# Last two weight units of each stage taken row by row, small extractions moved behind the last product

## What is computed

```
def first_block(...):
    h = modulate(rmsnorm(x, g_norm1), sh1, sc1)
    ...
    o = concatenate([o_mla, o_ret], axis=-1) @ w_out
    x_new = x + gt1 * o
    x_new = x_new + gt2 * conv_ffn(modulate(rmsnorm(x_new, g_norm2), sh2, sc2), ...)
    return rmsnorm(x_new, g_final)
```

## Time and profile before

| | |
|---|---|
| median of 3 runs | 1185.05 us |
| lowest and highest run | 1183.73 and 1187.86 us |
| the profiled execution, its own time | 1186.22 us |
| its span, first to last instruction | 1184.4 us |
| mean granted TensorE clock | 0.990 of full speed |
| VectorE, ScalarE busy | 831.3 and 600.2 us |
| TensorE instructions | 7032 |

### The profile page before, as it was taken

One profiled execution on the slowest core, in us unless ns is written; L12 is line 12 of the kernel. 1 busy time (PEld: TensorE's weight loads), 2 busy tenths in 40 slices (PEclk: granted clock), 3 DMA queues, 4 the chain that ended last, 5 costly groups with the idle time before them and its releaser, 6 DMA issues.

```text
span 1184.4 us, 18112 instructions
## 1 busy us (share of the span) xinstructions
PE 1130.3 (95%) x7032; PEld 979.7 (83%) x7032; DVE 831.3 (70%) x899; ACT 600.2 (51%) x872; POOL 210.5 (18%) x164
## 2 busy tenths in 40 slices
PE   5899989999999998999989999998999998999997
PEld 1587758879999886899879999886878987999986
DVE  3796465778887968898666765966888778454533
ACT  4864354456655436444454444336556767444432
POOL 1037300005566302010001212200000000122200
PEclk9999999999999999999989999998999999999999
DMA  8685550148786886976547887874877334555551
GB/s 327 258 318 206 212 213 1 37 151 299 260 281 213 327 316 210 363 236 233 179 148 240 298 278 248 333 296 154 322 283 285 134 100 133 186 177 183 197 189 72
DMA packets 124303, 263.36 MB, mean 222 GB/s; under 512 B 8329, under 2 KB 76497, under 8 KB 114001
## 3 DMA queue, kind: packets, MB, share of 16 engines
q1 hardware_dynamic: 121553, 254.56, 60.8%
q0 software_dynamic: 2688, 7.95, 2.2%
HBM read 261.43 MB, written 1.05 MB: 222 GB/s over the span
## 4 chain that ended last, share of the span: by engine, by line
PE 78%; DVE 11%; ACT 4%; issue 3%; DMA 2%; SPq 1%; POOL 0%; DVEq 0%; ACTq 0%
PE ps L1843 23%; PE ps L1844 23%; PE ps L1845 23%; DVE wl L580 2%; DMA mod_w<-in_w_ada_dram 2%; PE ps L2136 1%; PE ps L2152 1%; ACT wh L1313 1%; PE ps L1878 1%; DVE vg L1108 1%; DVE acc L592 1%; DVE x L761 1%; DVE xn L757 1%; PE ps L2187 1%; PE ps L2195 1%
## 5 line engine op out<-in xcount | busy, mean ns | idle before, releaser
L580 DVE TENSOR_TENSOR wl<-raw,wh 128x2048 fp32r<-128x2048 f32 (+2 forms) x149 | 343.0, 2304 | 111.7 <-ACT wh L1313 111.0
L1843 PE MATMUL ps<-hh,wh 128*128 128x256 f32 (+1 forms) x1192 | 339.2, 285 | 7.2 <-DVE hl L738 3.4
L1313 ACT ACTIVATE wh<-raw 128x2048 fp32r<-128x2048 f32 (+2 forms) x148 | 279.0, 1890 | 130.9 <-DMA raw<-in_ffn_w_down_dram 53.1
L1844 PE MATMUL ps<-hl,wh 128*128 128x256 f32 (+1 forms) x1192 | 335.9, 282 | 0.0
L1845 PE MATMUL ps<-hh,wl 128*128 128x256 f32 (+1 forms) x1192 | 335.9, 282 | 0.0
L1843 PEld LDWEIGHTS ps<-hh,wh 128*128 128x128 f32 (+1 forms) x1192 | 225.0, 189 | 9.6 <-issue 5.7
L1844 PEld LDWEIGHTS ps<-hl,wh 128*128 128x128 f32 (+1 forms) x1192 | 225.0, 189 | 0.3
L1845 PEld LDWEIGHTS ps<-hh,wl 128*128 128x128 f32 (+1 forms) x1192 | 224.9, 189 | 0.2
L1843 PE MATMUL ps<-wh,hh 128*128 128x512 f32 (+1 forms) x352 | 138.8, 394 | 6.1 <-DVE hraw L732 2.5
L592 DVE SCALAR_TENSOR_TENSOR acc<-au,cs,acc 128x2048 f32<-128x2048 f32 x54 | 132.0, 2444 | 15.2 <-DMA acc<-in_ada_b_dram 9.8
L2595 POOL TENSOR_TENSOR gl<-hid,gh 128x256 f32 (+1 forms) x66 | 78.9, 1196 | 338.8 <-ACT gh L1640 338.8
(11 more groups left out here) (324 smaller groups left out, 1579.0 us busy)
## 6 DMA issues: line engine op xcount, KB each, us to landing
au<-in_ada_w_dram SPq DMA_DIRECT2D x48, 1024.0 KB, 6.2
raw<-in_ffn_w_gu_dram SPq DMA_DIRECT2D x88, 512.0 KB, 4.7
raw<-in_w_up_dram SPq DMA_DIRECT2D x44, 512.0 KB, 4.8
raw<-in_ffn_w_down_dram SPq DMA_DIRECT2D x44, 512.0 KB, 4.5
au<-in_w_ada_dram SPq DMA_DIRECT2D x18, 1024.0 KB, 6.3
raw<-in_a_w_in_dram SPq DMA_DIRECT2D x32, 512.0 KB, 5.4
raw<-in_w_down_dram SPq DMA_DIRECT2D x22, 512.0 KB, 6.3
raw<-in_w_in_dram SPq DMA_DIRECT2D x16, 512.0 KB, 6.7
```

The lines of the kernel that those rows point to most:

```text
L580: nc.vector.tensor_tensor(wl[:, u % RAW, 0:n], raw[:, u % RAW, 0:n], wh[:, u % RAW, 0:n].bitcast(F32), ALU.subtract).then_inc(lo_done, 1)
L1313: nc.scalar.activation(wh[:, u % RAW, 0:n], raw[:, u % RAW, 0:n], ACT.Copy).then_inc(hi_done, 1)
L1843: nc.tensor.matmul(to, lh, rh, start=start, stop=False, skip_group_check=True)
L1844: nc.tensor.matmul(to, lh, rl, start=False, stop=False, skip_group_check=True)
```

## The change

- **Last two units together.** `last_products` replaces `last_product`: the last two units are multiplied bank by bank, so that each of the four banks gets all its 12 products of both units in a row; a bank's end is signalled by `acc_done`. The slot of the first of the two units is released in the middle of the last bank.
- **Rows in turn.** VectorE and ScalarE take the first half of row 0 when its bank is done, then the second, add and normalise row 0, and then the same for row 1 (`gated_part`, `normed_stage`; `acc_square`, `normed_squares`). ScalarE converts the front of the next unit between the rows.
- **Extraction.** TensorE extracts columns and gates directly behind the last product at all five stage ends (`turn_rows`), and transposes row 0 without waiting for row 1; group 7's columns are no longer made within the second FFN. Banks are chosen anew for it, and a semaphore `acc_read` keeps the transposes out of banks still to be read.
- **Gates last.** VectorE takes the gates out of PSUM after the whole operand is evicted (`last_parts`), and the wait for them on TensorE stands ahead of the FFN's loop.
- **Moves of additions.** Group 8 starts three units later; its additions follow from unit 109. The addition behind unit 126 goes into the head loop of the second attention, in quarters. In both attention stages VectorE takes the low part of the next unit ahead of an eviction.

The core of the diff:

```diff
 _spread(9, [119, 120, 121, 122, 123])
 FOX_ADA = 8 * 9 + 5
-ADA_AFTER.update({126: [FOX_ADA + 1], 127: [FOX_ADA + 2]})
-
-EXTRACT_AFTER = {7: 1, 105: 7}
+ADA_AFTER.update({127: [FOX_ADA + 2]})
+
+EXTRACT_AFTER = {7: 1}
 
 EX_COLS = {"shift_scale": (0, 16), "gate_shift": (8, 16), "scale_gate": (0, 8)}
 
-EX_BANKS = {1: (6, 7, 0), 2: (0, 2, 3), 3: (0, 0, 0), 4: (4, 2, 3), 5: (6, 4, 5), 6: (0, 0, 0), 7: (7, 7, 7),
-            8: (5, 6, 7), 9: (0, 2, 3)}
-
-TURN_BANKS = [(4, 5, 6, 7), (1, 2, 3, 0), (0, 1, 0, 1), (0, 1, 6, 7), (0, 1, 6, 7), (0, 1, 6, 7), (4, 5, 6, 7),
+EX_BANKS = {1: (6, 7, 0), 2: (4, 2, 3), 3: (0, 0, 0), 4: (4, 6, 7), 5: (4, 6, 7), 6: (0, 0, 0), 7: (0, 0, 0),
...
+            def gated_part(t, i, slot, place, last_unit, bank=0, r=None):
+
+                if r is not None:
+                    dve.wait_ge(sq_done, SQ_NO[r, t, i] + 1)
+                elif (t, i) == (1, 1):
+                    dve.wait_ge(w_used, split_no(last_unit) + 1)
+                else:
+                    dve.wait_ge(acc_done, 3 * place + 2 * t + i + 1)
+                cc = halves[i]
+                return nc.vector.tensor_tensor(xn[:, t, cc], ps[:, bank + 2 * t + i, :], gate[:, slot, cc], ALU.mult)
+
+            def add_part(t, cc):
+
+                nc.vector.tensor_tensor(x[:, t, cc], x[:, t, cc], xn[:, t, cc], ALU.add).then_inc(x_ready, 1)
+
+            def normed_add(r, t, parts):
+
                 row_rstd(r, t)
                 for cc in parts:
                     nc.vector.scalar_tensor_tensor(x[:, t, cc], xn[:, t, cc], rs_of(r, t), x[:, t, cc], ALU.mult,
...
             head_norms(1)
             take(14)
-            evac_low(N_RET, hl, hh, (2,))
             take(15)
-            evac_low(N_RET, hl, hh, (3,))
+            evac_low(N_RET, hl, hh, (2, 3))
             take(16)
             take(17, True)
...
+            def last_gated(slot, place, last_unit, bank=0, r=None):
+
+                gated_part(1, 1, slot, place, last_unit, bank, r).then_inc(acc_read, 1)
+                dve.wait_ge(acc_read, place + 1)
+
+            def last_parts(r, n, group, then):
+
+                front_first(then)
+                extract_columns(group)
                 normalise(r, 1, halves)
-                front_first(then)
                 evac_low(n, hl, hh, (0, 1))
                 front_second(then)
                 evac_low(n, hl, hh, (2, 3))
-
-            both_rows(0, W_OUT + 3, 0, None, X_FF0, HEADS_BANK)
-            next_rows(R_FF0, N_FF0, 2, 18)
+                extract_gate(group)
+
+            def normed_stage(place, last_unit, slot, ry, r, n, group, then, bank=0):
+
+                gated_part(0, 0, slot, place, last_unit, bank, ry)
+                link(gated_part(0, 1, slot, place, last_unit, bank, ry))
+                normed_add(ry, 0, whole)
+                normalise(r, 0, whole)
+                gated_part(1, 0, slot, place, last_unit, bank, ry)
+                last_gated(slot, place, last_unit, bank, ry)
+                normed_add(ry, 1, halves)
+                last_parts(r, n, group, then)
...
-                    if h < 8:
-                        ada_quarter(FOX_ADA, h // 2)
+                    v = FOX_ADA + h // 8
+                    if h % 8 == 1:
+                        dve.wait_ge(au_loaded[v % 2], 16 * (v // 2 - 2))
+                        dve.wait_ge(acc_step, v - 8)
+                    ada_quarter(v, h % 8 // 2)
...
+            def normed_squares(ry, r, x_base, place, last_unit, then=None, bank=0):
+
+                acc_square(ry, 0, 0, place, last_unit, bank)
+                first_half(ry, 0, 0)
+                acc_square(ry, 0, 1, place, last_unit, bank)
+                halves_root(ry, 0, 0)
+                if r is not None:
+                    front_high(then)
+                    x_row(r, x_base + 1)
+                acc_square(ry, 1, 0, place, last_unit, bank)
+                first_half(ry, 1, 2)
+                acc_square(ry, 1, 1, place, last_unit, bank)
+                halves_root(ry, 1, 2)
+                if r is not None:
+                    x_half(r, 0, x_base + 2)
+                    x_half(r, 1, x_base + 3)
+
+            beta_no = {}
             links = [0]
 
...
+            def turn_row(n, t, src, place=None):
+
+                for b in range(4):
+                    if t == 0 and b == 2 and place is not None:
...
+                    for q in range(2):
+                        k = 4 * (b // 2) + b % 2 + 2 * q
+                        at = q * TOK + t * P
+                        ins = nc.tensor.transpose(ps[:, TURN_BANKS[n][b], at:at + P], src[:, t, k * P:(k + 1) * P],
+                                                  ident)
...
-            def last_product(u, hi, lo, k0, bank=0):
-
-                w_hi, w_lo = unit(u, D)
+            def last_products(u, hi, lo, k0, bank=0):
+
+                views = [unit(u, D)]
                 for t in range(NT):
                     for cb in range(2):
                         cc = slice(cb * HALF, (cb + 1) * HALF)
                         tt = slice(t * P, (t + 1) * P)
-                        for kk in range(2):
-                            ins = three(ps[:, bank + 2 * t + cb, :], hi[:, k0 + kk, tt], lo[:, k0 + kk, tt],
-                                        w_hi[:, kk, cc], w_lo[:, kk, cc], False, kk == 1)
-                        if (t, cb) in ((0, 1), (1, 0)):
+                        for n in range(2):
+                            if n == len(views):
+                                views.append(unit(u + 1, D))
+                            w_hi, w_lo = views[n]
+                            for kk in range(2):
+                                k = k0 + 2 * n + kk
+                                ins = three(ps[:, bank + 2 * t + cb, :], hi[:, k, tt], lo[:, k, tt], w_hi[:, kk, cc],
+                                            w_lo[:, kk, cc], False, (n, kk) == (1, 1))
+                            if (t, cb, n) == (1, 1, 0):
+                                ins.then_inc(w_used, 1)
+                        if (t, cb) != (1, 1):
                             ins.then_inc(acc_done, 1)
                 ins.then_inc(w_used, 1)
...
                 up_unit(f, u0 + 1, 0, 1)
+                pe.wait_ge(ex_taken, EX_BASE[(3, 6, 10)[f]])
                 with pe.Fori(0, 4) as i:
                     for b in range(1, 3):
                         for h in range(2):
...
                         up_unit(f, u0 + 2 * b + h, b, h, None, group)
                 if f in LOOP_GROUP:
...
                     pe.wait_ge(gl_done, NFF * f + 2 * j + 2 + CREDIT)
-                    acc_product(DOWN[f] + j, gh, gl, 2 * j, j == 0, False, None, 7 if f == 1 and j == 7 else None)
+                    acc_product(DOWN[f] + j, gh, gl, 2 * j, j == 0, False)
                 pe.wait_ge(gl_done, NFF * f + NFF + CREDIT)
-                last_product(DOWN[f] + NBLK - 1, gh, gl, NFF - 2)
-
-            def extract_then_turn(g, n):
-
+                last_products(DOWN[f] + NBLK - 2, gh, gl, NFF - 4)
+
+            def turn_rows(n, place, g):
+
+                if n in (N_FF0, N_KV, N_FF2):
+                    pe.wait_ge(xn_ready, XN_BASE[n] + 1)
                 extract(g)
+                turn_row(n, 0, xn, place)
                 pe.wait_ge(ex_taken, EX_BASE[g] + 1)
```

312 lines of the change are left out of this document (161 added, 151 removed).

## The result

The changed kernel took 1180.22 us (median of 7 runs, 1178.12 to 1182.3), the kernel before 1186.2 us beside it (7 runs, 1183.73 to 1187.86). The ratio is 0.9953, 95% interval 0.9941 to 0.9965: 5.6 us faster. The forecast was 1170.8 us with a range from 1167.5 to 1178, so the direction was right and the size was not. The time lies 9.4 us above the forecast, and of the forecast gain of 14.3 us 8.7 are missing (the kernel before came out at 1186.2 here, not at the 1185.05 that the forecast started from). The profiled execution has a span of 1179.3 us against 1184.4.

A forecast was written before the change was run, and what follows sets the result against it. TensorE, busy 95%, was taken as the bound, with time won at its waits or by shortening its list. Terms at six places summed to minus 14.3 us, giving 1170.8 us from the 1185.05 median; range 1167.5 to 1178.

The forecast's parts named there:

- VectorE catches up at the unit that now carries two, before its split is needed: Group 8's first two additions move later; VectorE recovers at the unit with two additions, so no cost was counted.
- D minus 1.5: Second FFN into keys: window from T (stage's last product ends) to next product 1.5 us shorter, at T+7.75.
- I expect full clock: minus 2.8: After gating block and second FFN: shorter gaps keep TensorE at full clock, 2.8 us less; bounds nothing and 2.8.
- C: Gating block into second FFN: next product at T+7.75, window 2.7 us shorter, with 0.45 added for the memset.
- E: Second attention into third FFN: next product at T+7.3, window 2.2 us shorter.
- the first (chance 0.2): Rival: the half clock stays, 2.8 us are not won, slower transposes lengthen C by 0.7: 1174.3 us; chance 0.2.
- Gates behind the operand: Gate copies leave the chain, hidden beside 11.2 us of products; without that cover they cost 1.3 at A, C and E.
- A: Attention output into first FFN: TensorE's own list bounds it; next product at T+6.85, window 1.5 us shorter.
- B: First FFN into gating block: next product at T+8.6, window 2.6 us shorter.
- The second of the two units: Last two units: second needed at T-9.8 instead of T-5.6, costing 1.65 at A, 0.8 at B, 0.85 at E.
- F: End of the program: last add ends at T+3.2 instead of T+4.2, minus 1.0 us.
- The quarters of the moved addition in the second attention: Addition moved out of the way at E runs as four quarters in the second attention: 0.2 us; bounds nothing or 2.35.

The follow-up runs named there:

- the last probe: Four idle TensorE products added behind the second FFN, on the best kernel (six edits, ratio 0.988): 0.9918, 1176.32 us.
- the undoing: GpSimd's memset after the gating block and second FFN waits until row 1 is normalised, against the changed kernel: ratio 0.9939, 1177.62 us.

## Why the prediction was wrong

- **"VectorE catches up at the unit that now carries two, before its split is needed"**: the step that failed, and the largest single piece of what is missing. The sum had nothing for it; the first profile shows 3.7 us of waits. I counted VectorE's time, not where the doubled addition's piece comes from nor what stands behind its issue in SyncE's queue. The piece was 2.37 us late, the queue held the weight sends, and the price showed six units later. With both additions at unit 109 the larger wait went in that run, and over all profiles the stretch was 2.3 us shorter on the mean; the rest I put down to the addition too many behind D, which no run took away by itself.
- **"D minus 1.5"**: measured +0.2 and -0.9 in two profiles. The memset cost 1.27 and 0.62 us, not 0.45, and the columns, 3.6 us at full clock, took longer at half. The 3.5 us out of the second FFN came to the tenth, but they were no full saving at D: there TensorE's list, with the columns at half clock, is nearly as long as the window (busy 8.68 of 9.54 us). Against the same kernel without the move, 2.5 at best.
- **"I expect full clock: minus 2.8"**: C gave its 2.3 back, D gave none and took about 1.1 more, and E lost 1.5 in one profile of two. That C came out full was partly luck: in four of the seventeen later profiles the half clock stood there again. Of the rivals the first (chance 0.2) came nearest, though not as priced. Apart from D, the place of the half clock is a matter of the single execution; I took one profile's clock at C for a property of C. The Trainium skill (TensorE: Matmul & The Clock Gate, HAM oscillation) has idle gaps bring the half clock back, and I let it say that shorter gaps "can only help". In the last probe the clock fell with no gap since T; so that rule, as I used it, does not cover D.
- **"Gates behind the operand"**: right at A, C and E, worth 3.0 us together in the windows of the run that undid it, less than 1.3 each. At B their wait stands not ahead of an FFN loop but ahead of the second pair of units, 1.18 us. I had read one rule for five places; the fifth had other banks.
- **"The second of the two units"**: 1.65 forecast at A, 1.35 measured; 0.85 at E, 0.91 measured. At B 0.8 forecast, none in thirteen of the sixteen profiles with these units block by block, and 0.89 to 1.66 in three. And the price could be had back: the reason for it, "ScalarE's high part waits for the evictions", was an order in a list, not a need.
- **Right**: the windows at A (6.85 minus 0.44), B (8.6), C (7.75 plus 0.27), E (7.3 plus 0.28) and F (-1.0, measured -0.9). The chain behind T ran as worked out, gate half, add, front, row 1. The memset's 0.45 at C was 0.48 by the undoing. By the Trainium skill's second rule (GPSIMD Engine Reference, Key points: two SBUF inputs) the split front would have been slowed, by my estimate 0.8 us each at C and D; it was not. At D it ended before the memset began. At C it met the memset for 0.7 us and took 1.22. At B it lay beside one for its whole length and took 1.22 us too, as at D without one. The trace of the kernel before could have told it: there a whole split had a memset beside it for 1.7 us and took its usual 2.3:

```profile
451.34 1.83 POOL L2603 MEMSET acc<- 128x2048 f32 x1
451.62 1.22 DVE L684 TENSOR_TENSOR wl<-raw,wh 128x1024 fp32r<-128x1024 f32 x1
```

```profile
794.45 1.81 POOL L2518 MEMSET acc<- 128x2048 f32 x1 [36.81 <-PE ps L1878]
...
794.58 2.28 DVE L580 TENSOR_TENSOR wl<-raw,wh 128x2048 fp32r<-128x2048 f32 x1
```

- **The quarters of the moved addition in the second attention** (0.2): no wait in that loop is longer than before, but the loop takes 31.86 us against 31.60, so about what was forecast.

So the sum was right for the stage ends without D and wrong for what the change put elsewhere: 3.7 in the projections, 1.2 for the gates in the gating block, 1.7 at D, and some 3 of clock (1.6 behind D against the forecast, 1.5 behind E).

## What to carry to other kernels

Work moved out of a gap is costed where it goes, in each list and queue it enters: for an addition that means the transfer of its operand, and what a single ordered queue holds behind the issue of that transfer. Buffers named anew make new waits; go through every reader of every renamed bank. And a clock read in one execution is no property of a place: take a second profile of the same program before a term of the sum rests on it.
